# Second-half norms before the first expert row, other places for wq and the rows, two moved weight splits

## The reference

```
q = (ht @ wq).reshape(T, 8, 2, 128)
s = einsum('thcd,hcnd->thcn', q, subkeys)
s1, i1 = top_k(s[:, :, 0], 16);  s2, i2 = top_k(s[:, :, 1], 16)
cand = s1[..., :, None] + s2[..., None, :]          # 256 candidates per token and head
sc, ci = top_k(cand, 16);  e = expert index of each;  g = softmax(sc)
z = einsum('thkd,td->thk', take(u, e), h)           # 128 experts per token
a = gelu(z) * g
out = einsum('thk,thkd->td', a, take(v, e))
```

## Time and profile before

| | |
|---|---|
| median of 3 runs | 1326.41 us |
| the profiled execution, and its span | 1325.02 us, 1323.2 us |
| TensorE busy (matmul) | 1164.9 us, 88% of the span |
| VectorE, ScalarE, GpSimd busy | 69%, 38%, 25% of the span |
| bytes moved, mean rate | 405.68 MB, 307 GB/s |
| chain that ended last | TensorE 44%, DMA 29%, VectorE 15%, ScalarE 7% |

### The profile page before, as it was taken

The page is one execution under the profiler, slowest core; times in us unless marked ns, Lnnn a source line. Parts: engine busy times, 40 slices in busy tenths (PEclk is TensorE's granted clock), DMA queues, the critical chain, the costliest instruction groups (busy, mean ns, idle before and its releaser), DMA issues.

```text
span 1323.2 us, 15407 instructions
## 1 busy us (share of the span) xinstructions
PE 1164.9 (88%) x5438; PEld 823.1 (62%) x5438; DVE 912.1 (69%) x1874; ACT 503.5 (38%) x974; POOL 328.8 (25%) x310
## 2 busy tenths in 40 slices
PE   5889999999769998998788978777887999999999
PEld 5878888999645544443333433333333897899887
DVE  5875687788567877767776767776754686766544
ACT  4554534455332321222221222221423467555432
POOL 4000000000214655455444455444540100000000
PEclk9999999999979999999898999899998999999999
DMA  9753367686679999999999999999996541454551
GB/s 363 293 214 142 122 226 273 222 324 248 257 292 413 426 426 425 427 427 426 427 426 426 427 427 427 427 427 426 428 427 261 184 153 65 159 188 163 205 197 45
DMA packets 57697, 405.68 MB, mean 307 GB/s; under 512 B 6908, under 2 KB 7108, under 8 KB 9108
## 3 DMA queue, kind: packets, MB, share of 16 engines
q0 software_dynamic: 38576, 272.49, 49.1%
q1 hardware_dynamic: 19044, 132.19, 26.6%
HBM read 403.61 MB, written 1.05 MB: 306 GB/s over the span
## 4 chain that ended last, share of the span: by engine, by line
PE 44%; DMA 29%; DVE 15%; ACT 7%; issue 4%; POOL 1%; SPq 0%; DVEq 0%; ACTq 0%; POOLq 0%
DMA gbuf<-in_peer_uv,ei 17%; PE bank L827 12%; DMA ring<-in_peer_uv,ei 10%; DVE half L1498 4%; PE bank L479 4%; PE bank L475 4%; PE bank L476 4%; ACT half L1044 4%; PE bank L750 3%; PE bank L1018 2%; PE bank L1020 2%; PE bank L1019 2%; DVE gbuf L1924 2%; DMA ring<-in_weights 1%; PE bank L490 1%
## 5 line engine op out<-in xcount | busy, mean ns | idle before, releaser
L827 PE MATMUL bank<-gbuf,dg 128*128 128x512 f32 x584 | 278.5, 623 | 43.4 <-ACT dg L1319 43.4
L1498 DVE TENSOR_TENSOR half<-ring,half 128x1024 fp32r<-128x1024 f32 x175 | 212.7, 1223 | 137.4 <-ACT half L1044 136.9
L1924 DVE CUSTOM_DVE_ANT_0 gbuf<-gbuf,h2t 128x1024 f32<-128x1024 f32 x146 | 178.8, 1225 | 89.0 <-DMA gbuf<-in_peer_uv,ei 87.9
L827 PEld LDWEIGHTS bank<-gbuf,dg 128*128 128x128 f32 x584 | 115.1, 200 | 194.0 <-issue 138.6
L2253 POOL DMA_INDIRECT gbuf<-in_peer_uv,ei x146 | 171.9, 1177 | 253.8 <-PE bank L827 133.9
L827 PE MATMUL bank<-ring,dg 128*128 128x512 f32 x376 | 188.7, 648 | 47.2 <-ACT dg L1319 47.2
L1044 ACT ACTIVATE half<-ring 128x1024 fp32r<-128x1024 f32 x175 | 182.6, 1051 | 96.0 <-PE bank L1020 45.6
L827 PEld LDWEIGHTS bank<-ring,dg 128*128 128x128 f32 x376 | 75.1, 205 | 150.6 <-issue 86.4
L1311 ACT ACTIVATE za<-za 128x4 f32<-128x4 f32 x62 | 12.7, 205 | 407.0 <-DVE za L1924 407.0
L1924 DVE CUSTOM_DVE_ANT_0 ring<-ring,h2t 128x1024 f32<-128x1024 f32 x94 | 115.0, 1225 | 62.7 <-DMA ring<-in_peer_uv,ei 62.6
L2253 POOL DMA_INDIRECT ring<-in_peer_uv,ei x94 | 113.5, 1208 | 128.6 <-PE bank L827 93.4
(11 more groups left out here) (428 smaller groups left out, 1866.6 us busy)
## 6 DMA issues: line engine op xcount, KB each, us to landing
ring<-in_weights SPq DMA_DIRECT2D x114, 1024.0 KB, 4.9
gbuf<-in_weights SPq DMA_DIRECT2D x3, 1024.0 KB, 9.0
wq_place<-in_weights SPq DMA_DIRECT2D x3, 1024.0 KB, 8.8
gbuf<-in_peer_uv,ei POOLq DMA_INDIRECT x146, 21.8
bcs<-in_b_ada POOLq DMA_DIRECT2D x3, 512.0 KB, 9.8
ring<-in_peer_uv,ei POOLq DMA_INDIRECT x94, 21.0
xs<-in_x SPq DMA_DIRECT2D x2, 512.0 KB, 8.1
ya<-in_weights SPq DMA_DIRECT2D x1, 1024.0 KB, 17.2
```

The costliest lines, as they stand in the source:

```text
L827: r = e.matmul(acc[a][j][:, :], dg[:, i % 4, :], expert_rows(i)[:, 1024 + 512 * j:1536 + 512 * j], start=h == 0 and k == 0, stop=h == 7 an ...
L1498: e.tensor_tensor(l, v, h.bitcast(f32), ALU.subtract).then_inc(*o.inc(s_lov, split(n)))
L1924: e.tensor_tensor_reduce(row, row, h2t[:, ITS[n][0], :], 1.0, 0.0, ALU.mult, ALU.add, za[:, n % 2, i % 16:i % 16 + 1]).then_inc(*o.inc(s_d ...
```

## The change

- **Entry, VectorE:** half 1's norms stand ahead of `dot(0)`. The first weight comes after row 4, no longer after row 3.
- **Entry, ScalarE and TensorE:** the first gelu stands ahead of the second query part's copy, and the scores of head 0 for half 1 are done after row 0's product; their copy follows the first four diagonals.
- **Places:** wq's loads go to four `gbuf` places and two `wq_place`s. The third `wq_place` is a fifteenth place for rows. Rows 0 to 2 start in two ring slots and in it. The load of `g3` goes behind wq's. `WO_B` swaps chunks 7 and 4.
- **Late rows:** from row 236 on the rows turn in 11 places, so the two first ring slots are free for q2's loads.
- **Exit:** `hi(WQ0 + 16)` and `lo(WQ0 + 16)` move behind `experts_square(1)` and into `experts_norm(1)`; the later two splits move back too. TensorE does `block_features(1)` ahead of all of q2.

The core of the diff:

```
-    JOIN = {8: 11, 12: 12, 22: 13, 30: 8, 46: 9, 62: 10}
-    ROW_SLOT, turns = [], list(range(8))
+    JOIN = {8: 11, 9: 12, 22: 13, 30: 7, 46: 8, 62: 9, 78: 10}
+    ROW_SLOT, turns = [], [4, 5, 14, 0, 1, 2, 3, 6]
...
+        if i == 236:
+            turns = [j for j in turns if j < 12]
...
-    places += [gbuf[:, j, :] for j in range(5, 8)] + [wq_places[j][:, :] for j in w_free]
+    places += [gbuf[:, j, :] for j in range(4, 8)] + [wq_places[j][:, :] for j in w_free[0:2]]
...
-    WO_B = (3, 5, 6, 7, 4, 0, 1, 2)
+    WO_B = (3, 5, 6, 4, 7, 0, 1, 2)
... TensorE
-        pb = bank(2)
-        e.wait_ge(s_q, Q_DONE[0, 1])
-        half_scores(0, 1, pb, 0).then_inc(*o.inc(s_score, SC_DONE[0, 1]))
+                if i == 0:
+                    pb = bank(2)
+                    e.wait_ge(s_q, Q_DONE[0, 1])
+                    half_scores(0, 1, pb, 0).then_inc(*o.inc(s_score, SC_DONE[0, 1]))
...
-        cs_.append(split_done(chunk_at["q2", 0]))
-        q2_half(0, 0, 1)
         block_features(1, (2, 3))
-        cs_.append(split_done(chunk_at["q2", 1]))
-        q2_half(0, 1, 2)
-        q2_half(1, 0, 2)
-        for i in range(2, 4):
+        for i in range(4):
... ScalarE
-        first_query(1, 1)
-        e.wait_ge(s_score, SC_DONE[0, 1])
-        e.activation(sct[:, 0, 2:4, :], ...)
...
                 gelu(g)
+                if g == 0:
+                    first_query(1, 1)
                 for i in range(4 * g, 4 * g + 4):
                     diagonal(i)
+                if g == 0:
+                    e.wait_ge(s_score, SC_DONE[0, 1])
+                    e.activation(sct[:, 0, 2:4, :], ...)
...
-            if i == 254:
-                hi(WQ0 + 16)
         load_sqrt()
         experts_square(1)
+        hi(WQ0 + 16)
+        block_square(1)
         hi(WQ0 + 17)
-        block_square(1)
-        hi(WQ0 + 18)
         for g in range(2):
             features_hi(1, g, banks[2 + g], "h3")
+        hi(WQ0 + 18)
... VectorE: half 1's norms move ahead of the loop over the rows
-            if i < LAST and i % 4 == 3:
-                weight(i // 4)
+            if i < LAST and i % 4 == 3 and i > 3 or i == 4:
+                weight(i // 4 if i > 4 else 0)
...
-        lo(WQ0 + 16)
         for j, _ in enumerate(experts_norm(1)):
             if j == 3:
-                lo(WQ0 + 17)
+                lo(WQ0 + 16)
+        lo(WQ0 + 17)
... GpSimd
-            elif ROW_SLOT[i] in (0, 1, 2, 3, 7, 11):
+            elif ROW_SLOT[i] in (4, 5):
+                e.wait_ge(s_lov, split(WO0 + (5, 7)[ROW_SLOT[i] - 4]))
+            elif ROW_SLOT[i] == 6:
+                e.wait_ge(s_tr, TR["sk", 3])
+            elif ROW_SLOT[i] == 14:
+                e.wait_ge(*wo_done(7))
+            else:
                 e.wait_ge(s_chunk, WQ0)
-            else:
-                e.wait_ge(s_tr, TR["sk", 3])
... SyncE
-            if i == I_WQ + 5:
+            if i == I_Q2:
                 e.wait_ge(*wo_done(4))
                 e.dma_start(g3[:, :], ...)
...
-            elif I_WQ + 5 <= i < I_Q2:
-                e.wait_ge(*wo_done(i - I_WQ))
+            elif I_WQ + 6 <= i < I_Q2:
+                e.wait_ge(*wo_done(i - I_WQ - 1))
```

More of the change, by code:

```diff
@@ L18 @@
 NB = 3
-NG = 14
+NG = 15
 NGB = 8
@@ L223, in build_program @@
     ROW_BEFORE = [max((j for j in range(i) if ROW_SLOT[j] == ROW_SLOT[i]), default=None) for i in range(256)]
-    SLOT_HEAD = {12: 0, 13: 1, 8: 2, 9: 3, 10: 4}
+    SLOT_HEAD = {12: 0, 13: 1, 7: 2, 8: 3, 9: 4, 10: 5}
     def landed(i):
@@ L390, in build_program @@
     w_free = [(WO0 + 5 + j) % NB for j in range(3)]
-    places += [gbuf[:, j, :] for j in range(5, 8)] + [wq_places[j][:, :] for j in w_free]
+    places += [gbuf[:, j, :] for j in range(4, 8)] + [wq_places[j][:, :] for j in w_free[0:2]]
     row_places = [gbuf[:, j, :] for j in range(4)] + [ring[j][:, :] for j in UV_SLOTS] + [gbuf[:, j, :] for j in range(4, 8)]
-    row_places += [row_place[:, :], ring[A0][:, :], ring[A1][:, :]]
-    WO_B = (3, 5, 6, 7, 4, 0, 1, 2)
+    row_places += [row_place[:, :], ring[A0][:, :], ring[A1][:, :], wq_places[w_free[2]][:, :]]
+    WO_B = (3, 5, 6, 4, 7, 0, 1, 2)
     wo_hi = wo_halves[2::2] + [yh[:, 4:8, :].rearrange("p a b -> p (a b)"), wo_halves[0]]
@@ L807, in tensor_program @@
             query(f, slice(128, 256))
-        pb = bank(2)
-        e.wait_ge(s_q, Q_DONE[0, 1])
-        half_scores(0, 1, pb, 0).then_inc(*o.inc(s_score, SC_DONE[0, 1]))
-        frees[2] = ((s_sct, SC_DONE[0, 1]),)
         acc = [[bank(4 + 2 * a + j) for j in range(2)] for a in range(2)]
@@ L831, in tensor_program @@
                 r.then_inc(*o.inc(s_comb, i + 1))
+                if i == 0:
+                    pb = bank(2)
+                    e.wait_ge(s_q, Q_DONE[0, 1])
+                    half_scores(0, 1, pb, 0).then_inc(*o.inc(s_score, SC_DONE[0, 1]))
+                    frees[2] = ((s_sct, SC_DONE[0, 1]),)
                 for g in QUERY_AT.get(i, ()):
@@ L1283, in scalar_program @@
         first_query(1, 0)
-        first_query(1, 1)
-        e.wait_ge(s_score, SC_DONE[0, 1])
-        e.activation(sct[:, 0, 2:4, :], banks[2][:, 0:256].rearrange("p (a b) -> p a b", a=2), AF.Copy).then_inc(
-            *o.inc(s_sct, SC_DONE[0, 1]))
         def scores(h):
@@ L1359, in scalar_program @@
                 gelu(g)
+                if g == 0:
+                    first_query(1, 1)
                 for i in range(4 * g, 4 * g + 4):
                     diagonal(i)
+                if g == 0:
+                    e.wait_ge(s_score, SC_DONE[0, 1])
+                    e.activation(sct[:, 0, 2:4, :], banks[2][:, 0:256].rearrange("p (a b) -> p a b", a=2), AF.Copy).then_inc(
+                        *o.inc(s_sct, SC_DONE[0, 1]))
                 if g in EXP_AFTER:
@@ L1996, in vector_program @@
         tokens_done(0)
+        for j in range(2):
+            output_gained(1, j)
+        output_norm(1)
+        tokens_norm(1)
+        tokens_scale(1)
         norm0 = experts_norm(0)
@@ L2004, in vector_program @@
                     rt = route(n_rt)
-            if i == 0:
-                for j in range(2):
-                    output_gained(1, j)
-                output_norm(1)
-            elif i == 1:
-                tokens_norm(1)
-            elif i == 2:
-                tokens_scale(1)
-            elif i == 12:
+            if i == 12:
                 tokens_done(1)
-            if i < LAST and i % 4 == 3:
-                weight(i // 4)
+            if i < LAST and i % 4 == 3 and i > 3 or i == 4:
+                weight(i // 4 if i > 4 else 0)
             if i == 233:
```

## The result

| | before | after |
|---|---|---|
| median, taken in turn on one chip | 1326.05 us (1325.19 to 1327.83, 4 runs) | 1302.84 us (1301.56 to 1304.02, 4 runs) |
| ratio after to before | | 0.9823, interval 0.9806 to 0.984 |
| profiled execution, and its span | 1325.02 us, 1323.2 us | 1302.74 us, 1300.9 us |
| row 255's dot starts | 1007.41 | 991.66 |
| from there to k2's first matmul | 30.82 | 24.28 |

The change takes 23.2 us off the median and 22.3 off the profiled execution; 1304.6 was forecast.

What follows compares the result with a forecast made beforehand. From 402 to 1000 us the DMA engines, full at 426 GB/s, were taken as the bound, leaving gains only at the stream's ends. Entry 16.8 plus exit 5.0 made 21.8 us, so a 1304.6 us median, range 1300.5 to 1313.5.

Steps and rivals of the forecast that it cites:

- When the stream starts: Entry: row 0 issued at 350.3, wq's loads and g3 out of the way, stream starting at 352.1 not 358.9; 6.8 us.
- The hole: Entry: DMA standstill from 381 to 390 (9.0 us) and shortfall to 402 (2.0) go, less 1.0 for small holes.
- The whole entry: Start of the rows' stage: stream start, hole and shortfall less small holes, 16.8 us, bounds 13.4 and 17.8.
- That the stream leads, not the products: Entry: the DMA stream of rows, not the chain up to row 0's product, sets the gain; entry 16.8 us.
- the strongest rival: Products lead: holes at rows 16 to 31 eat the difference; entry 13.4, exit 3.0, 1310.0 us; chance 0.19.
- Exit: From row 255 to k2: 8.7 us sooner at row 255's end, 5.0 us left by k2, bounds 3.0 and 6.9.
- the first term: Exit: row 255's product follows row 254's without idle time and takes 1.8 us; its end 8.7 us sooner.
- The mechanism of the exit: Exit: row 255's gelu no longer waits for q2's load, so TensorE goes straight on, 6.7 us sooner.
- The clock: Exit: without six early q2 matmuls TensorE idles 5.0 us, so features(1) takes 3.75 instead of 2.02 us.
- Eleven late places: Rival, from row 236: too few rows in flight, 3.1 us a row, 13 us lost, 1317.6 us; chance 0.05.
- The slowing by the clock: Rival, rows' stage: too many rows at the low clock make TensorE bound it, 1366 us at 50% slow; chance 0.03.
- All goes well: Rival, both ends: entry 17.8 and exit 6.9, 1301.7 us; chance 0.10.

Runs made afterwards that it cites:

- late_wq_loads: Changed kernel, but wq's last two loads and g3 wait for all of half 1's w_out products, so 2.6 MB stand in the first rows' way; 1309.43 us.
- busy_exit_entry: Changed kernel with 18 unused matmuls on TensorE ahead of the exit's features(1) and 22 more ahead of the entry's features(1); 1302.78 us.
- split_before_last_gelu: Changed kernel with only ScalarE's first q2 split put back ahead of row 255's gelu; 1306.45 us.
- norms_behind_rows: Changed kernel with half 1's norms put back between the first rows' dots on VectorE; 1309.11 us.
- changed_again: The changed kernel unaltered, run once more on another chip, where the kernel before took 1325.14 us; 1304.50 us.
- two-by-two: Four kernels, old or new exit order with late or early first q2 load; exits 34.2 (old, late), 24.9 (old, early), 25.8 (new, late), 24.5 us (new, early).
- exit_order_old: Changed kernel with the old order of splits and q2 at the exit, the freed places kept; 1305.70 us.
- busy_exit: Changed kernel with 18 matmuls whose result nobody uses (idle products) on TensorE between row 255's product and features(1); 1302.05 us.
- norms_first_on_old: Kernel before, with only half 1's norms moved ahead of row 0's dot and the first weight after row 4; 1316.38 us.
- exit_old_late_load: Changed kernel with the old exit order, and q2's first load waiting for row 254's product as before; 1310.97 us.
- thirteen_late_places: Changed kernel without the cut to 11 places at row 236, so the last rows turn in 14 places; 1304.02 us.
- third group: Follow-up runs on one chip with the kernel before (1325.14 us) beside them; the changed kernel took 1304.5 us there.

## Why the prediction was right, and where it was off

**When the stream starts (6.8 us forecast).** The place and the cause were right. Row 0 was issued at 350.45 (350.3), with the loads out of the way, and late_wq_loads shows that loads in the rows' way cost about their length. What was mis-sized is the rate at the start: I let the stream run at 426 GB/s from 352.1 on. From 352 to 361 it moved 365, and 9 x (1 - 365/426) = 1.3 us are missing. With that, 6.8 - 1.3 + 9.0 + 2.0 = 16.5 us. Measured by the dots, rows 35 to 50 are 16.3 to 16.6 us sooner, and some 0.7 of it is lost later in the stage.

**The hole (9.0 + 2.0 - 1.0 us).** Right. features(1) came at 360.66 (360.6). Row 0's product came at 369.66, 2.1 sooner than the 371.8 of the forecast, because the query ahead of it ran at the full clock: its 32 matmuls took 3.81 us, where they took 5.83 before. That is luck of the execution: in seven of the nine copies with this entry the query took 5.7 to 6.1 us and the product came between 370.73 and 372.36. Row 16 was issued at 388.80 (390). Both came sooner than forecast and neither brought time, since the products have slack. The whole entry gave 15.75 instead of 16.8.

**That the stream leads, not the products.** This was the choice between the forecast and the strongest rival (entry 13.4). Neither late_wq_loads nor busy_exit_entry decides it, as said there. The copies with the same entry do. Row 0's product comes 19.2 us behind row 0's issue in the changed kernel's two traces and 21.2 to 21.5 in the seven others, and the dot follows 641.2 to 642.3 us behind the issue in all: in split_before_last_gelu the product is 2.0 us later than after and the dot on the same mark (641.25 against 641.21). With norms_behind_rows, where the product is 23.75 behind the issue, a hole opens and the dot moves by 2.5. So the products have a slack of some 2 us, and beyond it, by this one trace, they lead. The stretches agree: from 361 on the changed kernel moves 416 GB/s or more. And rows 35 to 50 are 16.4 us sooner after the change, not the 15.5 by which row 0's product moved.

**Exit (5.0 us forecast, 6.54 measured).** By its terms: row 255's product ends 25.61 us sooner, 9.86 beyond the entry's gain, where 8.7 was forecast. From there to features(1) it is 5.21 us (5.0). features(1) takes 3.75 us (3.75). From its start to k2 it is 14.88 us (15.2). So the first term was off most, by 1.2 us, the others by 0.2 and 0.3, and the first is a matter of the run: it depends on how far TensorE is behind when the rows end. Between 974 and 982 the clock differs from one profiled execution to the next:

```profile
974.64 3.49 PE L825 MATMUL bank<-gbuf,dg 128*128 128x512 f32 x4 [1.86 <-ACT dg L1313]
...
995.32 1.88 PE L825 MATMUL bank<-gbuf,dg 128*128 128x512 f32 x4
```

These are changed_again's, where row 244 took 3.49 us instead of 1.98, and row 255's product starts 1.45 later than after, at 995.32. The forecast's term, with the entry gain as measured, has it at 1010.96 - 15.75 = 995.21. Its exit, 25.29 us, would be a gain of 5.7.

**The mechanism of the exit was half right.** I said that row 255's gelu no longer waits since the split is moved. The two-by-two shows that the freed places do the same by themselves; had I worked out that load's landing for the old order too, I would have seen it. In exit_order_old it was issued at 988.7 and had landed at 993.6, so row 255's gelu came at 994.57, some 2 us late, where it was 9 us late with the late load. TensorE's backlog hid the 2 us there, and little of the 9.

**The clock.** features(1) took 3.75 us as forecast, and busy_exit took the 1.73 us back. The forecast's reason holds only in part. It said that q2's six early matmuls had kept TensorE going. But of the four traces that have them, with 3.3 to 3.8 us idle behind them, two show features(1) in 2.02 us (before, and norms_first_on_old) and two in 3.38 and 3.75 (exit_order_old and exit_old_late_load).

```profile
1018.55 2.02 PE L520 MATMUL bank<-masks,h2t 128*128 128x128 f32 x16 [3.59 <-DVE masks L1533]
```

Without them, and 5.0 to 5.8 us idle, it took 3.48 to 3.76 us in all seven. With 18 idle products and 1.2 us idle or less it took 2.02 in all three. So the old order gave the high clock in some executions only, and the price of giving it up, 1.73 us against this one trace of the kernel before, is less on average. How much less, four traces don't say.

**The other rivals.** Eleven late places cost nothing (thirteen_late_places). The slowing by the clock did not occur: the granted clock is 0.96 from 402 to 984, against 0.95 before. "All goes well" at 1301.7 lies nearer to the measured 1302.84 than it should by its own argument, because neither of its conditions was met: the clock at the exit was low, and the entry gave 15.75 and not 17.8. In the third group the changed kernel took 1304.5, close to the forecast of 1304.6, so the nearness of either number is in part luck.

## What to carry to other kernels

Where one resource is full for most of the time, look for what it does in the few microseconds ahead of the stage: loads that are issued late stood in the way of the stream for about their length here, and belong into its last idle stretch. A wait on an in-order engine costs what is queued behind it, so either move what is behind it ahead, or bring the awaited thing sooner; both together add little, and gains measured on the old kernel (8 us for the norms) are not those on the new one (2 by the trace, more by the medians). When a forecast rests on a clock level read from one trace, read it from several: the same instructions with nearly the same idle time ran at either level here. Some idle products in the wait gave 2.85 us by the medians.

## What the runs showed of the hardware

**The end of a gathered stream.** In the last 6 us of the rows the DMA engines are nearly idle: 29 GB/s from 986 to 988, a share of 0.07, about one engine of 16, and before the change 30 GB/s from 1001 to 1007. Yet the dots still come 2.44 us apart, each released by its row's landing. That would fit if most engines had moved their parts of the last rows, and the rows waited for the part of one that lagged; no row here shows the engines one by one, so this is argued and not shown. I had taken the end of the full rate for the end of the rows; 6 us lie between.

**The start of a gathered stream.** From 352 to 361 the stream moved 365 GB/s, with a DMA share of 0.97: the engines counted as busy, but moved less. In the other copies with this entry it was 332 to 407 GB/s at a share of 0.92 to 0.99. The cause stays open.

**When the clock rises.** In the entry of the changed kernel the low level ends 3 us after features(1) has begun, of the kernel before 8.4 us after the same 16 matmuls had begun (370.89). The rows, of after and of before:

```profile
360.60:363.60 3.00, 2.94 (x14) 2.97 (x15) 3.00 (x5) 0.60 (x1) 1.55 (x2) 0.50 0.99 412
364.00:370.00 6.00, 4.32 (x35) 3.95 (x34) 3.38 (x7) 5.20 (x11) 0.51 (x1) 1.00 1.00 416
```

```profile
370.90:379.30 8.40, 7.67 (x34) 7.40 (x35) 1.15 (x3) 3.02 (x6) 0.00 (x0) 0.50 1.01 425
```

TensorE had been idle for 6.22 us ahead of the one and 16.58 ahead of the other. That isn't the cause: busy_exit has the changed kernel's entry, instruction for instruction, with features(1) at 360.65 after the same 6.22 us, and its low level lasts some 5 us longer:

```profile
360.60:368.50 7.90, 7.11 (x32) 6.88 (x33) 5.88 (x11) 2.88 (x5) 1.55 (x2) 0.50 1.01 425
```

In norms_behind_rows, after 10.55 us idle, the level is high again 4.3 us after features(1) has begun (1.00 from 368.6 on). So the low level lasted 3 to some 9 us here, and the idle time ahead of it doesn't tell how long.
